# A two-layer hybrid trunk on one core: buffers on multiples of 128 bytes, head norms by Ln and Exp, a scan in another order

## The chip, the cores and the metric

The kernel runs on 1 of the 8 cores of a Trainium2 chip. The metric is the device time of one execution in microseconds, the median of several runs. Its engines: TensorE (PE; PEld are its weight loads), VectorE (DVE), ScalarE (ACT), GpSimd (POOL), SyncE (SP), which issues nearly all DMAs.

## What is computed

The reference has 256 latent and 256 context tokens of width 1,024 (here T = 512 columns, feature-major), and two layers. Each layer is `h += g1 * mixer(modulate(rms_norm(h)))`, then `h += g2 * relu(u @ w1)^2 @ w2`, with shift, scale and gate from `silu(c) @ w_mod`. Cut to what matters here:

```python
# layer 0 mixer: Fourier groups beside a bidirectional Mamba-2 scan, 4 groups g of 6 heads r, chunks of 128 tokens
cb     = einsum("bclgn,bcsgn->bclsg", cc, bc)                 # C.B of a chunk, shared by a group's heads
y_diag = einsum("bclsgr,bcsgrp->bclgrp", cb[..., None] * decay, xdt)
states = einsum("bcsgn,bcsgrp->bcgrpn", bc, xdt * decay_to_end[..., None])
h      = h * chunk_decay + state                              # carried over the chunks, both directions
y_off  = einsum("bclgn,bcgrpn->bclgrp", cc, h_enter) * exp(a_cum)
y      = rms_norm_per_group((y_diag + y_off + d_skip * xs) * silu(z)) * norm_g
out    = concatenate([fourier, y]) @ w_out                    # 2,048 -> 1,024
# layer 1 mixer: windowed attention and neighbourhood attention on projections, after
q, k   = rms_norm(q, per head of 64), rms_norm(k, per head of 64)
```

## The kernel before, in words

A script (`script()`) writes down a list of steps; every engine walks the same list and emits its own part of each step, so that the list is the order of every engine's queue. Between the engines stand counted semaphores. Every engine works strictly in this order, and a step whose wait isn't met holds up all that stands behind it on its engine.

*Products.* A float32 product is done as three passes of rounded halves: `w_hi*x_hi + w_hi*x_lo + w_lo*x_hi`. A weight tile is 1,024 x 128 (8 k tiles), so a product is 24 matmuls of 128x128 on 512 or 256 columns (`product`, L1506; the first two of a stage run interleaved by k in `pair_product`, L1513). SP loads tile u into `raw`, ScalarE copies it to `w_hi` (L839), VectorE subtracts for `w_lo` (L1094), both two products ahead, as the first thing of a product's step. The layer's input stands in `a_hi`/`a_lo`, the second operand (hidden values, second half of the mixer) in `b_hi`/`b_lo`. Results go to two PSUM banks in turn.

*Layer 0.* Projections of group 0 and the Fourier tiles, then the scan, group by group (163 to 525 us in the trace). In a group, eight slots (`slot(n)`) hold one product each, five of the next group's convolution inputs and three of z; in group 3, which has no successor, z in slots 0 to 2, nothing in slot 3, and then the output products outA 0 to 3. Around the slots stand the steps of the scan. `toks` turns tokens to rows (L1679, L1680). `cb` makes C.B of one chunk (L1694) and VectorE multiplies it with both masks into `cbm` (L1306). `seg` is the decay of one direction: six transposes (L1703), six Relu and one Exp into `ey` on ScalarE (L983, L986), times `cbm` on VectorE (L1312). `state`: GpSimd scales `xw` (two buffers, L827), TensorE multiplies (L1688), VectorE carries it on in `hent` (L1296, or L1298 and L1301). `yoff` takes the entering state (L1715; L1323, L1328), `y` the diagonal part (L1728, L1732), `yt` takes y down into `mixF` (L1338). `ysum`, `yrec`, `yrow`, `ynorm` normalise the group before (L1741, L995, L1352, L1749, L1360). Work of a convolution (taps L1242, L1245; L965; L1258) is placed by `gemm()` ahead of the next slot. States, cb, ysum, yoff and the head statistics take the PSUM banks 3 and 7 in turn (`B_AUX`), each only after its last user has been read.

*Mixer splits.* `mixF` has 16 tiles: 4 Fourier tiles and 3 of each group. `("mixsplit", 0)`, in the first turn of group 3, makes `a_hi`/`a_lo` of tiles 0 to 7 in one go (L1018, L1370), `("mixsplit", 1)`, after outA 6, `b_hi`/`b_lo` of tiles 8 to 15.

*Layer 1.* 18 projection products, q on 256 columns (8), k and v on 512 (5 each) (991 to 1089 us). Behind each, one slot later, `hstat`: a matmul sums the squares of a head (L1806), ScalarE takes `Sqrt` (L1002), VectorE the reciprocal (L1349); two slots later `hnorm` multiplies (L1425), and three later `rot` and, once, `dup` (L1827, L1440), the doubling of the window keys. Then attention, output product, MLP.

*MLPs.* Four passes of 8 ff1 products on `a` and 8 ff2 products on `b`: 512 columns in layer 0, 256 in layer 1.

*Buffers.* `place()` puts one buffer after another, each rounded up to 32 bytes, from byte 16512. `c0` is 8,224 bytes long, so that what follows it begins at 32 over a multiple of 128.

## Time and profile before

| | |
|---|---|
| median of 3 runs | 1374.86 us (1373.34 to 1379.74) |
| the profiled execution, its time | 1377.91 us |
| its span | 1376.1 us |
| granted TensorE clock, mean over the span | 0.961 |
| busy: PE, PEld | 1268.3 us, 1009.4 us |
| busy: DVE, ACT, POOL | 772.6 us, 506.3 us, 79.2 us |

The median says what the kernel takes; the profile is of one execution and says where. Its span runs from the first to the last instruction, and its own time is 1.8 us longer. TensorE's granted clock has two levels, 1 (2.4 GHz) and one half; a stretch's figure is the mean. A busy engine's time is counted as pieces, and matmuls overlap, so that busy time doesn't say how much could be saved; the waits do.

### The profile page before, as it was taken

The page shows a single profiled execution, that of the slowest core. Times are in us where ns is not written, and L with a number is a line of the kernel's source. Part 1 is how long each engine was busy: PE and PEld are TensorE (multiplying, and loading weights), DVE is VectorE, ACT ScalarE, POOL GpSimd, SP SyncE. Part 2 cuts the span into 40 slices and gives each one's busy share as a digit, 9 for nine tenths or more (in the row PEclk, how much of TensorE's full clock was granted, in tenths as well). Part 3 has the DMA queues.
Part 4 walks back from the last instruction along what each step waited for, and adds up shares of the span by engine and source line. Part 5 has one row for each costly group of instructions (what it writes and reads, how often), then busy time and mean ns, then how long its engine had stood idle before and what let it go on. Part 6 is the DMA issues. An engine that isn't in the chain of part 4 may idle for free.

```text
span 1376.1 us, 18731 instructions
## 1 busy us (share of the span) xinstructions
PE 1268.3 (92%) x7212; PEld 1009.4 (73%) x7212; DVE 772.6 (56%) x1203; ACT 506.3 (37%) x879; POOL 79.2 (6%) x70
## 2 busy tenths in 40 slices
PE   5799889899899899899999999999799799899998
PEld 1566667677677787677777777777587558899998
DVE  2644368586685555364353353343465796757664
ACT  2431144363444532341122122221543485534442
POOL 0000000101001002300000000004100002100000
PEclk9899999899899999899999999999899899999999
DMA  9456011111011112343444353443133202355553
GB/s 385 167 210 256 19 47 61 46 47 61 32 61 47 42 66 83 135 145 124 160 160 160 122 182 140 146 157 136 59 105 130 75 2 80 140 180 184 181 181 125
DMA packets 41531, 166.56 MB, mean 121 GB/s; under 512 B 4480, under 2 KB 6656, under 8 KB 38400
## 3 DMA queue, kind: packets, MB, share of 16 engines
q1 hardware_dynamic: 41040, 164.45, 33.5%
q10 hardware_dynamic: 432, 1.32, 0.2%
q8 instruction: 38, 0.62, 0.2%
q14 instruction: 21, 0.17, 0.0%
...
## 4 chain that ended last, share of the span: by engine, by line
PE 75%; DVE 12%; ACT 6%; issue 3%; DMA 3%; SPq 0%; DVEq 0%; ACTq 0%
PE ps L1506 53%; PE ps L1513 8%; PE ps L1529 3%; ACT ey L983 1%; DVE cacc L1245 1%; PE ps L1703 1%; DVE sm L1458 1%; DMA raw<-in_w_ff 1%; PE ps L1669 1%; DMA mring<-in_w_mod 1%; PE ps L1728 1%; PE ps L1715 1%; ACT u L889 1%; DMA xload<-in_ctx 1%; PE ps L1732 1%
## 5 line engine op out<-in xcount | busy, mean ns | idle before, releaser
L1506 PE MATMUL ps<-a_hi,w_hi 128*128 128x512 f32 (+1 forms) x880 | 330.2, 375 | 0.0
L839 ACT ACTIVATE w_hi<-raw 128x1024 fp32r<-128x1024 f32 x206 | 217.2, 1056 | 281.6 <-DMA raw<-in_w_ff 217.7
L1506 PE MATMUL ps<-a_hi,w_lo 128*128 128x512 f32 (+1 forms) x880 | 314.6, 357 | 0.0
L1506 PE MATMUL ps<-a_lo,w_hi 128*128 128x512 f32 (+1 forms) x880 | 314.5, 357 | 0.0
L1094 DVE TENSOR_TENSOR w_lo<-raw,w_hi 128x1024 fp32r<-128x1024 f32 x206 | 253.1, 1229 | 87.7 <-ACT w_hi L839 86.8
L1506 PEld LDWEIGHTS ps<-a_hi,w_hi 128*128 128x128 f32 x880 | 168.9, 192 | 38.3 <-ACT hr L1038 7.5
L1506 PE MATMUL ps<-b_hi,w_hi 128*128 128x512 f32 (+1 forms) x560 | 193.9, 346 | 0.0
L1506 PE MATMUL ps<-b_hi,w_lo 128*128 128x512 f32 (+1 forms) x560 | 192.0, 343 | 0.0
L1506 PE MATMUL ps<-b_lo,w_hi 128*128 128x512 f32 (+1 forms) x560 | 191.3, 342 | 0.0
L1506 PEld LDWEIGHTS ps<-a_lo,w_hi 128*128 128x128 f32 x880 | 168.7, 192 | 26.2 <-issue 2.6
L1506 PEld LDWEIGHTS ps<-a_hi,w_lo 128*128 128x128 f32 x880 | 168.0, 191 | 24.6
L1506 PEld LDWEIGHTS ps<-b_hi,w_hi 128*128 128x128 f32 x560 | 105.2, 188 | 23.0 <-issue 10.0
L1506 PEld LDWEIGHTS ps<-b_hi,w_lo 128*128 128x128 f32 x560 | 105.1, 188 | 13.9
L1506 PEld LDWEIGHTS ps<-b_lo,w_hi 128*128 128x128 f32 x560 | 105.2, 188 | 12.9
L1408 DVE SCALAR_TENSOR_TENSOR hT<-ps,mod,hT 128x256 f32<-128x256 f32 x96 | 43.3, 479 | 105.0 <-PE ps L1506 104.8
L1397 DVE TENSOR_TENSOR hq<-hr 128x512 f32<-128x512 f32 (+1 forms) x64 | 35.5, 555 | 103.3 <-ACT hr L1038 103.2
L1038 ACT ACTIVATE hr<-ps 128x512 f32<-128x512 f32 (+1 forms) x64 | 31.3, 488 | 161.8 <-PE ps L1506 115.6
L1513 PE MATMUL ps<-a_hi,w_hi 128*128 128x512 f32 (+1 forms) x192 | 70.1, 365 | 14.6 <-DVE a_lo L1184 12.5
L983 ACT ACTIVATE ey<-ps,acum 128x128 f32<-128x128 f32 x192 | 52.9, 374 | 53.9 <-PE ps L1703 53.3
L1529 PE MATMUL ps<-mring,sil 128*32 128x384 f32 (+1 forms) x448 | 57.3, 594 | 16.3 <-DMA mring<-in_w_mod 8.5
L1513 PE MATMUL ps<-a_lo,w_hi 128*128 128x512 f32 (+1 forms) x192 | 67.4, 351 | 0.0
L1513 PE MATMUL ps<-a_hi,w_lo 128*128 128x512 f32 (+1 forms) x192 | 67.1, 350 | 0.0
...
## 6 DMA issues: line engine op xcount, KB each, us to landing
raw<-in_w_ff SPq DMA_DIRECT2D x128, 512.0 KB, 3.4
...
```

The source lines that it names most:

```text
L839: nc.scalar.activation(w_hi[:, u % RING, :, :], raw[:, u % RING, :, :], ACT.Copy).then_inc(hi_done, 1)
L889: nc.scalar.activation(u32[:, f % 2, SEQ * i:SEQ * i + SEQ], nt[:, f % 2, SEQ * i:SEQ * i + SEQ], ACT.Identity, bias=mod[:, st[1], sh, i:i ...
L983: nc.scalar.activation(ey[:, di, r, :], ps[:, b + r // 3, P * (r % 3):P * (r % 3) + P], ACT.Relu, scale=-1.0, bias=acum[:, st[3], head_col ...
L1038: nc.scalar.activation(hr[:, m % 2, 0:ntok], ps[:, b, 0:ntok], ACT.Relu)\
L1094: v.tensor_tensor(w_lo[:, u % RING, :, :], raw[:, u % RING, :, :], w_hi[:, u % RING, :, :].bitcast(F32), ALU.subtract).then_inc(lo_done, 1)
L1245: v.scalar_tensor_tensor(out=acc, in0=cpad[:, n % 2, :, w:w + SEQ], scalar=convwT[:, w, t:t + 1], in1=acc, op0=ALU.mult, op1=ALU.add).then ...
L1397: v.tensor_tensor(hq[:, m % 2, 0:ntok], hr[:, m % 2, 0:ntok], hr[:, m % 2, 0:ntok], ALU.mult).then_inc(hq_done, 1)
L1408: ins = v.scalar_tensor_tensor(out=hs, in0=ps[:, b, SEQ * i:SEQ * i + SEQ], scalar=mod[:, L, 5 * KT + m, i:i + 1], in1=hs, op0=ALU.mult, o ...
L1458: v.tensor_reduce(sm[:, 3, i % 3, :], ps[:, b:b + 2, :], AX, ALU.max).then_inc(signal(dve_seq), 1)
L1506: ins = mm(out_ap, w_[:, n % RING, k, :], x_[:, k, 0:ntok], start=(k == 0 and j == 0), stop=(k == KT - 1 and j == 2))
L1513: ins = mm(outs[i], w_[:, tiles_[i] % RING, k, :], x_[:, k, 0:ntok], start=(k == 0 and j == 0), stop=(k == KT - 1 and j == 2))
L1529: ins = mm(ps[32 * q:32 * q + 32, b, 0:width], sil32[:, kk, :], mring[:, slot, width * q:width * q + width], start=(kk == 0), stop=(kk == ...
```

## The change

- `place()` rounds to 128 bytes, and `pick` in `c0` is 32 wide, so that every buffer begins at a multiple of 128. `zt` shares the place of `mrow`.
- Head norm factors are `exp(-0.5 * ln(mean + eps))`, both on ScalarE, and not `Sqrt` and a reciprocal on VectorE.
- `cb` is one step a group: four matmuls into one bank, one pass on VectorE, at the end of the group before. `cbm` holds all four chunks.
- The six states stand in a row around `seg b`, all ahead of slot 1, on three banks (3, 7 and 6) and four `xw` buffers (two of them lie in `ycomb`). `ysum` takes bank 2. The last `yt` of a group stands ahead of slot 6.
- The mixer splits are a step for each tile. Tiles 0 and 1 of the first half go to a new buffer `mixE` on the place of `cpad` and `cacc`, and the products take a list of operands (`operands`, not shown).

```diff
-    pick = np.zeros((P, 2 * QUADS))
+    pick = np.zeros((P, PICK_W))
...
+PICK_W = 32
+C0_A = 4 * P + PICK_W
...
-        def states(n):
-            for d, ch in STATES[n:n + 2]:
+        def states(i, n):
+            for d, ch in STATES[i:i + n]:
                 s.append(("state", g, d, ch))
+
+        def mixsplits(half, *tiles):
+            if g == G - 1:
+                s.extend(("mixsplit", half, f) for f in tiles)
         ch = SCAN_F
         if g == 0:
             s += [("toks", g, c_) for c_ in ch]
-        s += [("cb", g, ch[0]), ("seg", g, "f", ch[0])]
+            s.append(("cb", g))
+        s.append(("seg", g, "f", ch[0]))
         slot(0)
         if g:
             s.append(("ysum", g - 1))
-        states(0)
+        states(0, 3)
         s.append(("seg", g, "b", ch[0]))
-        states(2)
+        states(3, 3)
         if g:
             s.append(("yrec", g - 1))
+        mixsplits(0, 0)
         slot(1)
         if g:
-            s.append(("yrow", g - 1))
-        states(4)
-        if g:
-            s.append(("ynorm", g - 1))
+            s += [("yrow", g - 1), ("ynorm", g - 1)]
+        mixsplits(0, 1)
         for n in range(NCH):
             if n < NCH - 1:
-                s += [("cb", g, ch[n + 1]), ("seg", g, "f", ch[n + 1])]
+                s.append(("seg", g, "f", ch[n + 1]))
+            mixsplits(0, *((), (4,), (6, 7), ())[n])
             if n:
                 s.append(("yt", g, ch[n - 1]))
             s.append(("yoff", g, ch[n]))
             slot(2 + n)
             if n < NCH - 1:
                 s.append(("seg", g, "b", ch[n + 1]))
+            mixsplits(0, *((), (5,), (), ())[n])
             s.append(("y", g, ch[n]))
-            if g == G - 1 and n == 0:
-                s.append(("mixsplit", 0))
+            mixsplits(0, *((2, 3), (), (), ())[n])
+        s.append(("yt", g, ch[-1]))
         slot(6)
-        s.append(("yt", g, ch[-1]))
         if g < G - 1:
             s += [("toks", g + 1, c_) for c_ in ch[:2]]
+            s.append(("cb", g + 1))
             slot(7)
             s += [("toks", g + 1, c_) for c_ in ch[2:]]
         s.append(("ygate", g))
...
     s.append(("ysum", G - 1))
     gemm("outA", 4)
     s.append(("yrec", G - 1))
+    mixsplits(1, 0, 1)
     gemm("outA", 5)
     s += [("yrow", G - 1), ("ynorm", G - 1)]
+    mixsplits(1, 2, 3)
     gemm("outA", 6)
-    s.append(("mixsplit", 1))
+    mixsplits(1, 4, 5)
     gemm("outA", 7)
+    mixsplits(1, 6, 7)
...
-        elif k in ("state", "cb", "ysum", "hstat"):
-            n_var += k in ("ysum", "hstat")
-            job(st, B_AUX[n_aux % 2], freed={"state": ("ent_done", nk), "ysum": ("var_done", n_var),
-                                             "hstat": ("var_done", n_var)}.get(k))
+        elif k == "ysum":
+            n_var += 1
+            job(st, B_TR, freed=("var_done", n_var))
+        elif k == "state":
+            job(st, (B_AUX + (B_Y,))[(nk - 1) % 3], freed=("ent_done", nk))
+        elif k == "cb":
+            job(st, B_AUX[0])
+        elif k == "hstat":
+            n_var += 1
+            job(st, B_AUX[n_aux % 2], freed=("var_done", n_var))
...
-                at[0] += (size + 31) // 32 * 32
+                at[0] += (size + 127) // 128 * 128
...
+        mrow_at = at[0]
         mrow = place("mrow", [P, MI0 * P])
+        zt = place("zt", [P, T], offset=mrow_at)
...
-        cbm = place("cbm", [P, 2, P])
+        cbm = place("cbm", [P, NCH, 2, P])
         ycomb = place("ycomb", [P, 2, GX])
+        mixE = place("mixE", [P, 2, 2, T], F32R, offset=at[0])
...
+        xws = [xw[:, 0, :], xw[:, 1, :], ycomb[:, 0, :], ycomb[:, 1, :]]
+        mix_hi = [mixE[:, 0, k, :] if k < 2 else a_hi[:, k, :] for k in range(KT)], [b_hi[:, k, :] for k in range(KT)]
+        mix_lo = [mixE[:, 1, k, :] if k < 2 else a_lo[:, k, :] for k in range(KT)], [b_lo[:, k, :] for k in range(KT)]
...
-                    if n >= 2:
-                        pool.wait_ge(*filled(st_l[n - 2]))
-                    pool.tensor_tensor(heads(xw[:, n % 2, :]), heads(xdt[:, di, ch, :]),
+                    if n >= 4:
+                        pool.wait_ge(*filled(st_l[n - 4]))
+                    if n % 4 >= 2 and g:
+                        pool.wait_ge(*filled(("y", g - 1, SCAN_F[-1])))
+                    pool.tensor_tensor(heads(xws[n % 4]), heads(xdt[:, di, ch, :]),
...
-                    nc.scalar.activation(rms_of(st), ps[:, b, 0:odd_tokens[st[1:]]], ACT.Sqrt, scale=1.0 / HD,
+                    nc.scalar.activation(rms_of(st), ps[:, b, 0:odd_tokens[st[1:]]], ACT.Ln, scale=1.0 / HD,
                                          bias=eps[:, 0:1]).then_inc(signal(var_done), 1)
+                    act.wait_ge(*latest())
+                    nc.scalar.activation(rms_of(st), rms_of(st), ACT.Exp, scale=-0.5).then_inc(signal(hs_done), 1)
                 elif k == "mixsplit":
-                    hi = (a_hi, b_hi)[st[1]]
-                    if st[1]:
-                        high(unit[early] + AHEAD)
-                    for last_read in readers(st):
-                        act.wait_ge(*last_read)
-                    for f in range(KT):
-                        t = KT * st[1] + f
-                        act.wait_ge(mix_done, t + 1)
-                        if st[1] == 1 and f == 0:
-
-                            act.wait_ge(mix_done, 2 * KT)
-                            for q in y_jobs(G - 1, SCAN_F[-1]):
-                                act.wait_ge(*filled(q))
-                        nc.scalar.activation(hi[:, f, :], mixF[:, t, :], ACT.Copy).then_inc(signal(mixhi_done), 1)
+                    _, half, f = st
+                    if st == ("mixsplit", 0, 0):
+                        act.wait_ge(xbc_done, 5 * G)
+                    elif st == ("mixsplit", 0, 2):
+                        act.wait_ge(*filled(("gemm", "z", G * XT - 1)))
+                    elif st == ("mixsplit", 1, 0):
+                        for q in y_jobs(G - 1, SCAN_F[-1]):
+                            act.wait_ge(*filled(q))
+                    act.wait_ge(mix_done, KT * half + f + 1)
+                    nc.scalar.activation(mix_hi[half][f], mixF[:, KT * half + f, :], ACT.Copy).then_inc(signal(mixhi_done), 1)
...
-                    v.tensor_tensor(cbm[:, :, :], ps[:, b, None, 0:P].broadcast_to([P, 2, P]), masks, ALU.mult).then_inc(freeing(st), 1)
+                    v.tensor_tensor(cbm[:, :, :, :], ps[:, b, :].rearrange("p (c l) -> p c l", c=NCH).unsqueeze(2).broadcast_to([P, NCH, 2, P]),
+                                    masks.unsqueeze(1).broadcast_to([P, NCH, 2, P]), ALU.mult).then_inc(freeing(st), 1)
...
-                elif k == "hstat":
-                    dve.wait_ge(var_done, rms_n[st])
-                    v.reciprocal(rms_of(st), rms_of(st)).then_inc(signal(rstd_done), 1)
...
-                    hi, lo = ((a_hi, a_lo), (b_hi, b_lo))[st[1]]
-                    if st[1]:
-                        low(unit[early] + AHEAD)
-                    for f in range(KT):
-                        t = KT * st[1] + f
-                        dve.wait_ge(mixhi_done, t + 1)
-                        dve.wait_ge(*latest())
-                        v.tensor_tensor(lo[:, f, :], mixF[:, t, :], hi[:, f, :].bitcast(F32), ALU.subtract).then_inc(signal(split_done), 1)
+                    _, half, f = st
+                    dve.wait_ge(mixhi_done, KT * half + f + 1)
+                    dve.wait_ge(*latest())
+                    v.tensor_tensor(mix_lo[half][f], mixF[:, KT * half + f, :], mix_hi[half][f].bitcast(F32), ALU.subtract).then_inc(signal(split_done), 1)
...
-                    dve.wait_ge(rstd_done, rms_n[("hstat",) + st[1:]])
+                    dve.wait_ge(hs_done, qk_n[st[1:]] + 1)
...
-                    _, g, ch = st
+                    g = st[1]
+                    pe.wait_ge(xbc_done, 5 * g + 2)
                     b = jobs[st][0]
                     if free_before[st]:
                         pe.wait_ge(*emptied(st))
-                    mm(ps[:, b, 0:P], xbc[:, g % 2, 0, P * ch:P * ch + P], xbc[:, g % 2, 1, P * ch:P * ch + P], start=True, stop=True).then_inc(filling(st), 1)
+                    for ch in range(NCH):
+                        ins = mm(ps[:, b, P * ch:P * ch + P], xbc[:, g % 2, 0, P * ch:P * ch + P], xbc[:, g % 2, 1, P * ch:P * ch + P], start=True, stop=True)
+                    ins.then_inc(filling(st), 1)
```

VectorE's instructions in the first turn of group 1, from state 4 on (`hent` the states, `ey` the decay, `rcol` yrec, `cacc` the taps of a convolution, `mixF` with `vec` ynorm), before:

```order
L1298 TENSOR_TENSOR hent<-hent,dt_tot 128x384
L1301 TENSOR_TENSOR hent<-hent,ps 128x384
L1352 RECIPROCAL rcol<-rcol 128x4
L1242 TENSOR_SCALAR cacc<-cpad,vec 128x512
L1245 SCALAR_TENSOR_TENSOR cacc<-cpad,vec,cacc 128x512 x4
L1094 TENSOR_TENSOR w_lo<-raw,w_hi 128x1024
L1298 TENSOR_TENSOR hent<-hent,dt_tot 128x384
L1301 TENSOR_TENSOR hent<-hent,ps 128x384
L1298 TENSOR_TENSOR hent<-hent,dt_tot 128x384
L1301 TENSOR_TENSOR hent<-hent,ps 128x384
L1360 SCALAR_TENSOR_TENSOR mixF<-mixF,vec,ps 128x512 x3
L1306 TENSOR_TENSOR cbm<-ps,c_55 128x256
```

and with the change, from the second decay on (states 1 to 3 stand ahead of it):

```order
L1342 TENSOR_TENSOR ey_87<-ey_87,cbm 128x768
L1327 TENSOR_TENSOR hent<-hent,dt_tot 128x384
L1330 TENSOR_TENSOR hent<-hent,ps 128x384
L1327 TENSOR_TENSOR hent<-hent,dt_tot 128x384
L1330 TENSOR_TENSOR hent<-hent,ps 128x384
L1327 TENSOR_TENSOR hent<-hent,dt_tot 128x384
L1330 TENSOR_TENSOR hent<-hent,ps 128x384
L1379 RECIPROCAL rcol<-rcol 128x4
L1271 TENSOR_SCALAR cacc<-cpad,vec 128x512
L1274 SCALAR_TENSOR_TENSOR cacc<-cpad,vec,cacc 128x512 x4
L1124 TENSOR_TENSOR w_lo<-raw,w_hi 128x1024
L1387 SCALAR_TENSOR_TENSOR mixF<-mixF,vec,ps 128x512 x3
```

Two of the six states stood behind the reciprocal, the taps and the w_lo of slot 1, and cbm of the next chunk behind them; now all six stand ahead of the reciprocal, and there is no cbm.

ScalarE in group 3, behind the zt of the second z product (`ey` the decays, `a_hi<-mixF` the splits), before:

```order
L941 ACTIVATE zt<-ps 128x512
L983 ACTIVATE ey_87<-ps,acum 128x128 x6
L986 ACTIVATE ey_87<-ey_87 128x768
L1018 ACTIVATE a_hi<-mixF 128x512 x8
L983 ACTIVATE ey_86<-ps,acum 128x128 x6
L986 ACTIVATE ey_86<-ey_86 128x768
L983 ACTIVATE ey_86<-ps,acum 128x128 x6
L986 ACTIVATE ey_86<-ey_86 128x768
L983 ACTIVATE ey_87<-ps,acum 128x128 x6
```

and with the change:

```order
L973 ACTIVATE zt<-ps 128x512
L1015 ACTIVATE ey_88<-ps,acum 128x128 x6
L1018 ACTIVATE ey_88<-ey_88 128x768
L1048 ACTIVATE a_hi<-mixF 128x512 x2
L1015 ACTIVATE ey_87<-ps,acum 128x128 x6
L1018 ACTIVATE ey_87<-ey_87 128x768
L1048 ACTIVATE a_hi<-mixF 128x512
L1015 ACTIVATE ey_87<-ps,acum 128x128 x6
L1018 ACTIVATE ey_87<-ey_87 128x768
L1048 ACTIVATE a_hi<-mixF 128x512
L1015 ACTIVATE ey_88<-ps,acum 128x128 x6
L1018 ACTIVATE ey_88<-ey_88 128x768
```

The eight splits stood in one block between two decays; now two stand there, and the others one or two behind each decay (two have gone ahead, to `mixE`).

ScalarE in the odd projections, a v product and the statistics of the q product before it, before:

```order
L839 ACTIVATE w_hi<-raw 128x1024
L954 ACTIVATE vT<-ps 128x512
L1002 ACTIVATE nt<-ps,eps 128x256
L839 ACTIVATE w_hi<-raw 128x1024
L945 ACTIVATE kT<-ps 128x512
L949 ACTIVATE sq<-ps 128x512
```

and with the change:

```order
L870 ACTIVATE w_hi<-raw 128x1024
L986 ACTIVATE vT<-ps 128x512
L1034 ACT_TABLE_LOAD
L1034 ACTIVATE nt<-ps,eps 128x256
L1037 ACT_TABLE_LOAD
L1037 ACTIVATE nt<-nt 128x256
L870 ACTIVATE w_hi<-raw 128x1024
L977 ACTIVATE kT<-ps 128x512
L981 ACTIVATE sq<-ps 128x512
```

One `Sqrt` has become a table load, an Ln, a table load and an Exp; so it is for all 13.

## Rows read from the trace of the kernel before

**Rows 1.** The page, engines: busy us, share of the span, instructions.
```profile
PE 1268.3 (92%) x7212; PEld 1009.4 (73%) x7212; DVE 772.6 (56%) x1203; ACT 506.3 (37%) x879; POOL 79.2 (6%) x70
```

**Rows 2.** Table by stretch: length, busy us of each engine (x instructions), granted clock, DMA share, GB/s.
```profile
163.00:247.00 84.00, 75.06 (x437) 60.16 (x438) 60.62 (x97) 37.31 (x85) 7.49 (x8) 0.98 0.14 47
247.00:333.00 86.00, 77.44 (x440) 62.03 (x439) 62.09 (x98) 40.08 (x85) 6.17 (x6) 0.94 0.15 52
333.00:420.00 87.00, 78.29 (x437) 62.55 (x436) 61.65 (x97) 40.06 (x85) 6.18 (x6) 0.92 0.14 48
420.00:525.00 105.00, 94.88 (x517) 76.05 (x516) 62.66 (x100) 48.84 (x94) 3.54 (x4) 0.95 0.17 58
...
991.00:1089.00 98.00, 90.62 (x459) 74.68 (x459) 63.90 (x61) 42.13 (x72) 0.00 (x0) 0.98 0.35 118
```

**Rows 3.** TensorE's waits, whole run: what waited <- releaser: us, times, longest.
```profile
PE ps L1694 <- DVE hent L1301: 11.7, 4, 3.7
...
PE ps L1679 <- DVE mixF L1338: 5.5, 3, 1.8
...
PE ps L1715 <- DVE cbm L1306: 4.7, 3, 1.6
PE ps L1688 <- ACT rcol L995: 4.6, 3, 1.5
PE ps L1703 <- ACT ey L983: 4.5, 1, 4.5
...
PE ps L1513 <- DVE hT L1104: 2.5, 1, 2.5
PE ps L1827 <- DVE kdup L1440: 2.5, 1, 2.5
```

**Rows 4.** Timeline of TensorE, group 1: start, us, engine, line, operation [idle before <-releaser].
```profile
268.79 1.46 PE L1688 MATMUL ps<-xw,btok 128*128 128x384 f32 x4
273.87 0.80 PE L1694 MATMUL ps<-xbc 128*128 128x128 f32 x2 [3.63 <-DVE hent L1301]
...
275.74 1.32 PE L1715 MATMUL ps<-hent,xbc 128*128 128x384 f32 x2
```

**Rows 5.** Table by stretch, three short pieces; the granted clock stands ahead of the DMA share.
```profile
273.30:276.70 3.40, 2.83 (x11) 2.53 (x11) 3.16 (x6) 0.66 (x3) 0.00 (x0) 0.51 0.03 5
358.60:365.50 6.90, 6.05 (x17) 4.86 (x18) 5.68 (x10) 3.85 (x9) 0.00 (x0) 0.51 0.00 0
...
1044.70:1048.10 3.40, 3.40 (x11) 2.36 (x12) 1.56 (x2) 0.00 (x0) 0.00 (x0) 0.51 0.00 1
```

**Rows 6.** Timeline of TensorE, first MLP: 1st and 24th matmul of an a and a b product.
```profile
608.01 0.39 PE L1506 MATMUL ps<-a_hi,w_hi 128*128 128x512 f32 x1
...
613.22 0.39 PE L1506 MATMUL ps<-a_hi,w_lo 128*128 128x512 f32 x1
...
631.79 0.40 PE L1506 MATMUL ps<-b_hi,w_hi 128*128 128x512 f32 x1
...
637.16 0.40 PE L1506 MATMUL ps<-b_hi,w_lo 128*128 128x512 f32 x1
```

**Rows 7.** Table by stretch, one turn of group 1.
```profile
292.33:304.81 12.48, 10.90 (x73) 8.65 (x72) 11.39 (x19) 7.07 (x17) 0.00 (x0) 1.00 0.14 43
```

**Rows 8.** Groups by shape, VectorE: busy us, mean ns | idle before; one pass of a state.
```profile
L1301 DVE TENSOR_TENSOR hent<-hent,ps 128x384 f32<-128x384 f32 x16 | 8.9, 554 | 0.6
```

**Rows 9.** Timeline of ScalarE, group 3: the splits of the first half.
```profile
454.16 4.25 ACT L1018 ACTIVATE a_hi<-mixF 128x512 fp32r<-128x512 f32 x8
```

**Rows 10.** One line's instructions, the head reciprocals: shortest/median/longest ns.
```profile
L1349 DVE RECIPROCAL nt<-nt x13: 1743/1753/3353, 996.6 to 1085.9; 128x256 f32<-128x256 f32 x8, 128x512 f32<-128x512 f32 x5
```

**Rows 11.** Groups by shape, ScalarE: the table load of dt's Ln.
```profile
L903 ACT ACT_TABLE_LOAD x1 | 1.3, 1283 | 0.0
```

**Rows 12.** Timeline of ScalarE, odd projections: two k slots, each at its first copy.
```profile
1065.32 0.60 ACT L945 ACTIVATE kT<-ps 128x512 f32<-128x512 f32 x1 [3.50 <-PE ps L1506]
...
1071.64 0.60 ACT L945 ACTIVATE kT<-ps 128x512 f32<-128x512 f32 x1 [3.72 <-PE ps L1506]
```

44 lines of the change are left out of this document (24 added, 20 removed).

## The prediction

> **What bounds the kernel now.** I read the page first: TensorE is busy for 92% of the span [rows 1], so only what shortens its own work, or the time in which it waits, can pay. The table by stretch shows where it waits: in the scan (163 to 525 us, the four head groups) busy time falls short by some 36 us, in the odd projections (991 to 1089) by 7 [rows 2]. The list of TensorE's waits names the causes [rows 3]: in the scan the cb product waits 11.7 us in four waits for a state's copy on VectorE, the next group's transposes 5.5 us for the y tile, yoff 4.7 us for the cb bank, the states 4.6 us for ScalarE's ysum; later once 4.5 us behind the mixer splits, once 2.5 us at the start of outB, once 2.5 us at the doubling of the keys. The timeline shows the largest in its place in group 1 [rows 4], and pieces of time around such waits have a granted clock of 0.51 [rows 5]: the lower level, 1.2 instead of 2.4 GHz.
>
> **(a) Aligned buffers.** `a_hi`, `a_lo`, the weights and `hT` already began at multiples of 128 bytes; from `vec` on, nearly everything began 32, 64 or 96 bytes behind one, `b_hi` and `b_lo` by 32. In one pass of the first MLP an `a` product has 23 steps from 608.01 to 613.22, 226.5 ns each; a `b` product 23 steps from 631.79 to 637.16, 233.5 ns each [rows 6]. Shape, weights, clock and what the other engines do are alike, so I put the 7 ns on the buffer. It holds for 4 x 8 ff2 and 8 outB products of 24: 960 matmuls, 6.7 us, all on the path. The second MLP's 256-column products are paced by weight loads, whose buffers were aligned: nothing. For the other misplaced operands (mring, ey, hent, prob) no aligned twin stands in the trace; the bounds are nothing and, at 7 ns for some 400 wide ones, 3 us; I take nothing, as most are short. VectorE's and ScalarE's own times I leave as they are: they are off the path mostly, and between nothing and a gain there.
>
> The Trainium skill (SBUF — State Buffer, section Door 1, on the DMA port swizzle) gives SBUF lines of 16 bytes; 32 is a multiple of that, so by this rule the move changes nothing and the sum is 6.7 us smaller. Here [rows 6] speak against it.
>
> **(b) The scan.** Removed: the ysum bank ahead of the states (ysum now takes B_TR), the three cb products behind the states (cb is made once a group, ahead of slot 7 of the group before), yoff's wait for a cb bank, and the transposes' wait, as the last y tile is now taken down ahead of slot 6. These are the first four of [rows 3]: 11.7 + 5.5 + 4.7 + 4.6 = 26.5 us.
>
> What is late next? In group 1 yoff, with slot 2 behind it, began at 275.7, behind states 5 and 6 (268.8) and the 3.6 us wait [rows 4]. Now all six states stand ahead of slot 1. VectorE carries a state on with two passes of 0.55 us [rows 8], 3.3 us for the last three, which queue behind the second ey product. That product moves up by the 1.5 us that ysum cost, less the 0.7 of a third state; so VectorE is through at about 267, and with it the reciprocal that yrow needs. Slot 1 ends at about 266, so yrow may wait 1 us, and yoff starts at about 268: 7 to 8 us sooner. In the turns after that, TensorE was busy 10.9 us in the turn at 292 and waited the rest of 12.5 [rows 7]; VectorE's own turn by its widths (two ey 1.9, y 0.9, yoff 1.6, xbc 0.7, taps 3.7, w_lo 1.2) is 10.0, so the cover is thin. For yrow and such edges I put back 1.2 us a group, 4.8 us. The wide cbm is one pass of 1,024 columns for four of 256, no more than before and off the path; GpSimd's work is the same, only earlier, in four buffers.
>
> The clock: the pieces at 273.3 and 358.6 held 2.83 and 6.05 us of TensorE's work at 0.51 [rows 5]. They lie at the cb wait of group 1 and of group 2; without the wait I expect the full clock there, which gives half of that back, 4.4 us. Pieces at the states, where work is light with or without waits, I leave. Sum of (b): 26.5 - 4.8 + 4.4 = 26.1 us.
>
> **(c) Splits in pieces.** In group 3 eight a_hi copies, 4.25 us, stood between two ey steps on ScalarE [rows 9], and TensorE waited 4.5 us for the second. Now two stand there and one behind each ey. That turn has no product as cover: ey (some 2.5 us) and a split still come between two seg, so part stays; of 4.5 I take 2 us. At outB the last residual no longer queues behind eight b_lo passes: the wait of 2.5 us goes. The waits per tile inside the first pair are covered, as each k takes 6 matmuls, 1.4 us, and a split 0.5 us on ScalarE and 0.7 on VectorE.
>
> **(d) Head norm factors.** Removed: 13 reciprocals on VectorE of 1.75 to 3.35 us [rows 10]. Added on ScalarE: 13 exponentials of about 0.55 us and, by the order, a table load ahead of each Ln and each Exp, 26 of 1.283 us [rows 11] (one at the head of attention goes): 40 us on an engine busy 42 of 98 [rows 2]. It must be checked by slot. A k slot lasts 6.3 us and ScalarE idles 3.7 of it [rows 12]; 1.28 + 1.28 + 0.6 + 0.1 = 3.3 are added: it fits, with 0.4 to spare. A q slot lasts 3.3 us and ScalarE needs 5.2: it falls back by 1.9, in at most two slots in a row, and the v slot behind them and weights made two products ahead take that up. So I cost the loads at nothing, hidden by products. Gained on the path: the doubling of the keys queued behind a reciprocal, 1.2 us of the 2.5 go, and of the half-clock piece there (3.4 us [rows 5]) 0.6; ahead of attention a reciprocal of 3.35 and two norms become load, Ln, load, Exp and one norm, 0.7. Sum 2.5 us.
>
> The Trainium skill (ScalarE: Activation LUTs, section Table sets) has Ln and Exp in one set, so that Ln then Exp is one load; in this program the Ln of dt, behind an Exp, has its own load [rows 11], and the order shows one for each. By the page's 2.7 us a load, ScalarE would need 8.8 us in a k slot and bind it; the trace has 1.283.
>
> **Sum.** 6.7 + 26.1 + 2 + 2.5 + 2.5 = 39.8 us. The profiled execution took 1377.9 us (its span is 1376.1), which makes 1338; it lies 3.0 us over the median of the runs, 1374.9, so **1335 us**.
>
> **Rivals.** *R1, the buffers do nothing*: what makes `b` products slower would be something else in their place. For it, that no other row tells aligned from misplaced; against it, [rows 6]. 1335 + 6.7 = 1342. The rule on 16-byte lines above gives the same time. *R2, the waits only move*: VectorE, in strict order, becomes the bound where a turn has a convolution (10.0 us against TensorE's 10.5), and yrow or yoff inherits the wait for the last state. For it, the thin margin; against it, the reciprocals, cb and ysum no longer chain the engines. Half of (b) lost is 1348, all of it 1361. *R3, slower: the loads bind ScalarE in the odd projections.* Each slot would then wait for two loads and an Exp: 26 x 1.283 + 13 x 0.55 = 40.5 us in front of TensorE, and as TensorE waits in each slot, the stage's products (8 x 2.9 + 10 x 5.5 = 78 us) would run in part at the lower clock as in [rows 5]; half of them adds 39. 1335 + 40.5 gives 1376, with 10 to 39 for the clock 1386 to 1415. It decides where ScalarE needs more than a k slot's 6.3 us; I have 5.9. *R4, no such change*: the order shows all pieces in place, so only the clock could hide them; within R2.
>
> **How the numbers follow.** A measurement of this kernel can tell about 0.5% from no change: under 1368.0 is faster, over 1381.7 slower. Forecast 0.71, R1 0.10, R2 0.13, R3 0.04, other 0.02. All but R3 and the unnamed are faster, save a rest of R2 joined by a part of R3's waits: faster 0.91, same 0.04, slower 0.05. Low end: none of the 4.8 put back, the 3 us of (a), and 7 us more of clock: 1320. High end: R2 whole, 1360.
>
> **What would show it.** `b` products step at 227 ns, or (a) is wrong. TensorE's list has no wait of cb for hent and none of the transposes for mixF, and a group takes 75 to 79 us. In the odd projections ScalarE is busy over 75 us, yet no wait of TensorE ends in it. The forecast is wrong if a group still takes over 82 us, or if ScalarE ends TensorE's waits there.

## The result and the profile after

The changed kernel takes **1321.76 us**, median of 4 runs (1320.65 to 1324.72), the kernel before 1374.95 us. The ratio is 0.9607 with a 95% interval of 0.9589 to 0.9626: faster by 53 us, where the prediction had 40. The profiled execution took 1322.42 us, its span is 1320.6 us, and the granted clock is 0.974 on the mean.

The page of the changed kernel, engines, as [rows 1]:

```profile
PE 1245.9 (94%) x7212; PEld 1000.6 (76%) x7212; DVE 744.2 (56%) x1178; ACT 546.0 (41%) x917; POOL 79.3 (6%) x70
```

The number of matmuls is the same, and still TensorE is busy for 22 us less. That is the first sign of where the time came from: not from the waits alone.

The table by stretch of the changed kernel, with the columns of [rows 2]. The stretches are shifted so that each holds the same products as there: four groups of the scan, then the odd projections.

```profile
163.60:238.30 74.70, 73.13 (x443) 59.70 (x444) 61.34 (x95) 37.48 (x85) 9.11 (x10) 1.00 0.16 52
238.30:312.20 73.90, 72.74 (x440) 59.31 (x439) 61.91 (x95) 40.26 (x85) 6.29 (x6) 1.00 0.18 59
312.20:387.20 75.00, 73.60 (x437) 59.84 (x436) 61.23 (x94) 40.24 (x85) 6.33 (x6) 0.98 0.17 56
387.20:487.20 100.00, 94.50 (x519) 76.39 (x518) 62.34 (x99) 48.88 (x94) 2.03 (x2) 0.97 0.19 62
941.00:1035.80 94.80, 89.13 (x459) 73.49 (x459) 36.06 (x49) 80.58 (x108) 0.00 (x0) 1.00 0.37 122
```

Group 1 took 86.0 us and takes 73.9. Of these 12.1 us, waits are 7.4 (length less busy time: 8.56 before, 1.16 now), and 4.7 is busy time (77.44, now 72.74) for the same 440 matmuls, at a clock of 1.00 for 0.94. Group 2 shows the same: 12.0 us, 7.3 of them waits and 4.7 busy time. The prediction had a group at 75 to 79 us; these two take 73.9 and 75.0.

TensorE's waits in the changed kernel, whole run (what waited, the releaser, us, times, longest), as [rows 3]:

```profile
PE ps L1775 <- DVE rcol L1379: 3.7, 3, 1.4
...
PE ps L1729 <- ACT ey L1015: 1.6, 1, 1.6
PE ps L1758 <- DVEq L1360: 1.6, 1, 1.6
...
PE ps L1853 <- DVE kdup L1463: 0.8, 1, 0.8
```

The first four waits of [rows 3] are gone, 26.5 us. New are 3.7 us of yrow for the reciprocal, and in group 3, behind the first splits, 1.6 for the second ey (4.5 before) and 1.6 for VectorE's queue.

The pieces at half clock, between the scan's start and the end of outB. In the kernel before there were eight; the table of those pieces, without the two whose like stands in [rows 5] (273.4 to 276.8 and 358.7 to 365.5, busy 2.93 and 6.05 us):

```profile
188.00:191.40 3.40, 3.35 (x11) 2.75 (x12) 1.53 (x3) 1.18 (x5) 0.00 (x0) 0.50 0.00 0
256.30:263.10 6.80, 5.70 (x14) 3.71 (x15) 1.18 (x3) 3.63 (x9) 2.56 (x4) 0.50 0.00 0
...
341.60:348.40 6.80, 5.42 (x13) 3.52 (x14) 1.46 (x3) 3.63 (x9) 2.76 (x3) 0.50 0.02 4
...
430.40:433.80 3.40, 3.40 (x10) 2.18 (x9) 0.56 (x2) 0.94 (x4) 0.83 (x1) 0.50 0.00 0
457.70:464.50 6.80, 4.30 (x30) 3.57 (x30) 6.08 (x11) 5.59 (x16) 0.00 (x0) 0.50 0.00 0
525.90:529.40 3.50, 3.46 (x8) 2.81 (x9) 1.02 (x1) 0.53 (x1) 0.00 (x0) 0.51 0.00 0
```

and all that the changed kernel has there:

```profile
320.40:323.80 3.40, 3.40 (x9) 2.00 (x8) 2.60 (x4) 1.81 (x3) 2.11 (x2) 0.50 0.00 0
395.50:398.90 3.40, 3.40 (x9) 1.96 (x8) 3.10 (x5) 1.82 (x3) 2.03 (x2) 0.50 0.01 2
460.40:463.80 3.40, 3.40 (x9) 2.63 (x9) 1.22 (x1) 3.40 (x6) 0.00 (x0) 0.50 0.02 6
```

Eight pieces became three. TensorE's work in them was 34.6 us and is 10.2. At half clock work takes nearly twice its time (a step of 430 ns for 230 in gap_three, below), so that by estimate the pieces cost 17.3 us before and cost 5.1 now: 12.2 us won, where the prediction had 4.4. The three that are left have no wait ahead of them. Each begins 2.8 to 3.3 us after the start of a `ysum`, which is 24 matmuls of one column; the one ahead of 320.4 in the timeline:

```profile
317.12 2.73 PE L1767 MATMUL ps<-c,gate 128*128 128x1 f32 x24
```

Over the scan and outA as a whole (from product 9 to the middle of outB's first pair, with the wait in it) the two traces differ by 43.4 us, 27.5 of them waits and 15.9 busy time. Below, "scan and outA" is always this stretch.

A `b` product of the first MLP in the changed kernel, first and 24th matmul, as the lower half of [rows 6]:

```profile
587.22 0.39 PE L1529 MATMUL ps<-b_hi,w_hi 128*128 128x512 f32 x1
...
592.43 0.39 PE L1529 MATMUL ps<-b_hi,w_lo 128*128 128x512 f32 x1
```

23 steps in 5.21 us are 226.5 ns each, for 233.5 before.

ScalarE in a k slot of the odd projections, timeline of the changed kernel, as [rows 12]:

```profile
1018.41 0.60 ACT L977 ACTIVATE kT<-ps 128x512 f32<-128x512 f32 x1 [0.36 <-PE ps L1529]
1018.90 0.59 ACT L981 ACTIVATE sq<-ps 128x512 f32<-128x512 f32 x1
1019.51 1.28 ACT L1034 ACT_TABLE_LOAD   x1
1020.81 0.69 ACT L1034 ACTIVATE nt<-ps,eps 128x512 f32<-128x512 f32 x1
1021.52 1.28 ACT L1037 ACT_TABLE_LOAD   x1
1022.81 0.63 ACT L1037 ACTIVATE nt<-nt 128x512 f32<-128x512 f32 x1
1023.35 1.04 ACT L870 ACTIVATE w_hi<-raw 128x1024 fp32r<-128x1024 f32 x1
1024.76 0.60 ACT L977 ACTIVATE kT<-ps 128x512 f32<-128x512 f32 x1 [0.36 <-PE ps L1529]
```

The slot lasts 6.35 us and ScalarE idles 0.36 of it, where it idled 3.7: it fits, by a hair.

Following the products one by one through both traces, the changed kernel is ahead by 8.7 us behind group 0, 20.8 behind group 1, 32.8 behind group 2, 42.1 in the middle of outB's first pair, 44.1 at the first MLP, 50.0 at the odd projections, 55.1 at outO and 55.5 at the end of the span. At the start of the scan it is 1.3 us behind; half-clock pieces of the prologue lie otherwise there, as they do from kernel to kernel in all the runs below.

### The profile page after: what moved, and what is told of

The parts are those of the page before. It is cut to its first block, busy times and chain, and to the rows that moved or that the text cites. A ratio compares the mean times of both kernels' runs of the same rounds, so it can differ in the third digit from the quotient of the medians.

```text
span 1320.6 us, 18748 instructions
## 1 busy us (share of the span) xinstructions
PE 1245.9 (94%) x7212; PEld 1000.6 (76%) x7212; DVE 744.2 (56%) x1178; ACT 546.0 (41%) x917; POOL 79.3 (6%) x70
## 4 chain that ended last, share of the span: by engine, by line
PE 85%; DVE 7%; ACT 4%; DMA 3%; issue 2%; SPq 0%; DVEq 0%; ACTq 0%
PE ps L1529 59%; PE ps L1536 8%; PE ps L1552 3%; PE ps L1729 2%; PE ps L1754 1%; DVE sm L1481 1%; PE ps L1692 1%; DMA mring<-in_w_mod 1%; PE ps L1741 1%; PE ps L1711 1%; PE ps L1758 1%; ACT u L920 1%; PE ps L1767 1%; DMA xload<-in_ctx 1%; ACT ey L1015 1%
## 5 line engine op out<-in xcount | busy, mean ns | idle before, releaser
L1529 PE MATMUL ps<-a_hi,w_hi 128*128 128x512 f32 (+1 forms) x868 | 321.9, 371 | 0.0
L1529 PE MATMUL ps<-a_lo,w_hi 128*128 128x512 f32 (+1 forms) x868 | 308.9, 356 | 0.0
L1529 PE MATMUL ps<-a_hi,w_lo 128*128 128x512 f32 (+1 forms) x868 | 308.8, 356 | 0.0
L1529 PEld LDWEIGHTS ps<-a_hi,w_hi 128*128 128x128 f32 x868 | 165.2, 190 | 37.8 <-issue 8.5
L1529 PEld LDWEIGHTS ps<-a_lo,w_hi 128*128 128x128 f32 x868 | 165.2, 190 | 24.7 <-issue 1.0
L1529 PEld LDWEIGHTS ps<-a_hi,w_lo 128*128 128x128 f32 x868 | 164.9, 190 | 23.8
L1529 PEld LDWEIGHTS ps<-b_hi,w_lo 128*128 128x128 f32 x560 | 106.2, 190 | 12.2
L1536 PE MATMUL ps<-a_hi,w_hi 128*128 128x256 f32 (+1 forms) x188 | 68.6, 365 | 12.0 <-DVE a_lo L1214 11.9
L1552 PE MATMUL ps<-mring,sil 128*32 128x384 f32 (+1 forms) x448 | 57.9, 600 | 15.7 <-DMA mring<-in_w_mod 8.1
L1536 PE MATMUL ps<-a_lo,w_hi 128*128 128x256 f32 (+1 forms) x188 | 66.3, 352 | 0.0
L1536 PE MATMUL ps<-a_hi,w_lo 128*128 128x256 f32 (+1 forms) x188 | 66.0, 351 | 0.0
```

The source lines that it names most:

```text
L1529: ins = mm(out_ap, w_[:, n % RING, k, :], (x_[k][:, 0:ntok] if type(x_) is list else x_[:, k, 0:ntok]), start=(k == 0 and j == 0), stop=(k ...
L1536: ins = mm(outs[i], w_[:, tiles_[i] % RING, k, :], (x_[k][:, 0:ntok] if type(x_) is list else x_[:, k, 0:ntok]), start=(k == 0 and j == 0) ...
L1552: ins = mm(ps[32 * q:32 * q + 32, b, 0:width], sil32[:, kk, :], mring[:, slot, width * q:width * q + width], start=(kk == 0), stop=(kk == ...
```

## Experiments

All kernels below were timed against the kernel before, on one chip for each set. Where two of them are compared, it is by their ratios, 0.001 of which is 1.4 us; the changed kernel's ratio is 0.9607.

### a_alone: the buffers alone, on the kernel before

```diff
-                at[0] += (size + 31) // 32 * 32
+                at[0] += (size + 127) // 128 * 128
```

> The kernel before with every buffer rounded up to 128 bytes and nothing else changed. Theory (the buffers are worth the b products alone): b products step at 227 ns for 233.5, 960 x 7 ns = 6.7 us, so 1374.9 - 6.7 = 1368. Rival 1 (the scan's and the norms' operands also gained by their place, which would explain part of the 13 us that the change brought beyond my sum): 1355 to 1362. Rival 2 (the place of a buffer does nothing, the b products sped up for another reason): 1375, steps still 233.5.

Measured: 1371.16 us, ratio 0.9953 (0.9938 to 0.9968), so 6.5 us (4.4 to 8.5). A `b` product of the first MLP starts its first matmul at 629.87 and its 24th at 635.09, 227 ns a step. Both rivals fall: the buffers do something, and no more than that.

### a_offsets: three operands off the multiple, on the changed kernel

```diff
+        a_lo = place("a_lo", [P, KT, T], F32R, shift=96)
+        b_hi = place("b_hi", [P, KT, T], F32R, shift=64)
+        b_lo = place("b_lo", [P, KT, T], F32R, shift=32)
```

(`shift` adds to the buffer's place, the next one is rounded up to 128 again.)

> The changed kernel with three operands moved off a multiple of 128 bytes: a_lo by 96, b_hi by 64, b_lo by 32; a_hi stays. The trace shows each operand's own step. Theory 1 (anything off a multiple of 128 costs): matmuls on a_lo, b_hi and b_lo at 512 columns step at 233 to 234 ns, those on a_hi at 227; some 670 + 320 + 320 of them x 7 ns = 9.2 us, 1331. Theory 2 (a multiple of 64 is enough): b_hi stays at 227, a_lo and b_lo rise, 6.9 us, 1328.7. Theory 3 (these places do nothing): 1321.8.

Measured: 1327.47 us, ratio 0.9656 (0.9630 to 0.9681), 6.7 us more than the changed kernel. The same `b` product in its timeline:

```profile
589.49 0.40 PE L1529 MATMUL ps<-b_hi,w_hi 128*128 128x512 f32 x1
...
594.79 0.40 PE L1529 MATMUL ps<-b_hi,w_lo 128*128 128x512 f32 x1
```

230.4 ns a step; an `a` product has 231.3. So the third theory falls, and the first holds in its sign but not in its picture: the step isn't set by each operand's own place, since those on `a_hi`, which stayed at 0, slowed down with the others, and neither product reached 233.5. The second theory is not settled, because `b_hi` (64) and `b_lo` (32) slowed together.

What nobody had asked stands in the second MLP. With 256 columns, the `b` product numbered 200 takes 2.71 us for its 23 steps here, 117.8 ns each, as in the kernel before (117.7); in the changed kernel it has 120.0, and so it has in a_alone, where nothing but the places differs from the kernel before. **Off the multiple, the narrow products are faster.** From outO to the end a_offsets wins back 3.7 of the 7.8 us that it had lost.

### d_undone and d_double: the head norm factors

```diff
-  nc.scalar.activation(rms_of(st), ps[...], ACT.Ln, scale=1.0 / HD, ...)
-  nc.scalar.activation(rms_of(st), rms_of(st), ACT.Exp, scale=-0.5)
+  nc.scalar.activation(rms_of(st), ps[...], ACT.Sqrt, scale=1.0 / HD, ...)
+  v.reciprocal(rms_of(st), rms_of(st))
```

> The changed kernel with the head norm factors by Sqrt on ScalarE and a reciprocal on VectorE, as before. My sum had the change at 2.5 us, the two traces differ by 5.1 us over the odd projections and the head of attention (a wait of the doubling 1.7 shorter, one ahead of attention 0.6 shorter, the rest clock). Theory (all of that is the change of the factors): 1321.8 + 5.1 = 1327. Rival (my 2.5 us, the rest was the clock's luck): 1324. Rival (nothing, the loads cost what the reciprocals did): 1322.

Measured: 1330.3 us, ratio 0.9659 (0.9646 to 0.9672), 7.2 us more than the changed kernel. Its waits in the odd projections and ahead of attention:

```profile
PE ps L1868 <- DVE kT L1449: 5.0, 1, 5.0
PE ps L1854 <- DVE kdup L1464: 2.5, 1, 2.5
```

The doubling's wait is 2.5 us again, and a piece at half clock follows it (997.1 to 1000.5) that the changed kernel doesn't have. Followed by products, it falls behind by 3.2 us at this place and by 0.7 more up to outO. It is behind by 1.1 us already at the first MLP, with the same program up to there, because its trace has a piece at half clock behind the ysum in group 1, where the changed kernel's trace has none:

```profile
243.12 2.73 PE L1768 MATMUL ps<-c,gate 128*128 128x1 f32 x24
```

```profile
246.20:249.60 3.40, 3.40 (x8) 1.78 (x7) 2.33 (x5) 2.00 (x3) 1.78 (x2) 0.51 0.00 0
```

Some 3.9 us are the factors' own in the traces; 7.2 with an interval of some 3 us on either side is the runs' figure. The theory's 5 us lies within that, and both rivals lie below it.

```diff
   nc.scalar.activation(rms_of(st), rms_of(st), ACT.Exp, scale=-0.5)
+  nc.scalar.activation(rms_of(st), rms_of(st), ACT.Ln)
+  nc.scalar.activation(rms_of(st), rms_of(st), ACT.Exp)
```

> The changed kernel with a second Ln and a second Exp behind the first pair of each head statistic, same values: two more table loads and two more passes, 2 x 1.28 + 1.2 = 3.8 us more of ScalarE for each of the 13. Theory (the loads are hidden only as long as a slot has room: a k slot of 6.3 us had 5.9 in it, a q slot of 3.3 had 5.2): now k slots need 9.7, q slots 8.4 to 9.0, v slots 2.3, together some 127 us against a stage of 92, so 35 us slower and up to 20 more by the clock: 1357 to 1377, with the weights' w_hi ending TensorE's waits. Rival (ScalarE has plenty of room, its loads overlap with its other work): 1322 to 1326.

Measured: 1361.07 us, ratio 0.9884 (0.9867 to 0.9901), 38 us more. TensorE's waits in this stage:

```profile
PE ps L1836 <- ACT sq L981: 10.4, 5, 3.3
PE ps L1843 <- ACT vT L986: 8.1, 1, 8.1
PE ps L1871 <- DVE kT L1452: 7.5, 1, 7.5
```

The slots' arithmetic holds on both sides of its limit: at 5.9 us in a 6.3 us slot no wait of TensorE in the odd projections ends in ScalarE, and at 9.7 the stage grows by 36 us, where 35 and some clock had been worked out. A load is 1.283 us in every record of both kernels. The Trainium skill (ScalarE: Activation LUTs, section What ACT_TABLE_LOAD costs) makes its 2.7 us of a load of about 1.283 us and of a drain of about 1.38. The first figure agrees with the trace. The drain doesn't show: in the k slot above the load follows the Activate before it by 0.02 us, and the Ln follows the load as closely. The same page (section Table sets) has Ln and Exp in one set; here each Ln and each Exp has its own load.

### states_split: the states in their old places

```diff
-        states(0, 3)
+        states(0, 2)
         s.append(("seg", g, "b", ch[0]))
-        states(3, 3)
+        states(2, 2)
...
-            s += [("yrow", g - 1), ("ynorm", g - 1)]
+            s.append(("yrow", g - 1))
+        states(4, 2)
+        if g:
+            s.append(("ynorm", g - 1))
```

> The changed kernel with the states in their old places: two, two, and the last two behind yrow; cb once a group, the banks and all else stay. Theory 1 (the order of the states was what made the large wait, and waits draw half-clock pieces after them): the 11.7 us that cb waited for the last state come back at yoff, with 0.6 us of clock for each us waited (before against changed, TensorE's busy time over the scan fell by 13.5 us and its waits by 25.6), so +12 to +19: 1334 to 1341 on a chip where the changed kernel takes 1322. Theory 2 (the wait comes back without any clock): +12, 1334. Rival (the chain over cb's bank was the cause, the order does nothing): 1322 to 1325.

Measured: 1347.52 us, ratio 0.9797 (0.9775 to 0.9819), 26 us more. Its waits, and its group 1 in the table by stretch:

```profile
PE ps L1744 <- DVE hent L1333: 15.8, 4, 4.7
...
PE ps L1778 <- DVE rcol L1382: 2.3, 3, 0.8
```

```profile
243.70:325.60 81.90, 76.46 (x439) 61.55 (x437) 61.43 (x95) 40.18 (x85) 5.88 (x6) 0.94 0.16 52
```

With cb made once a group the wait for the last state simply passes to yoff, and is longer than it was (15.8 for 11.7). TensorE is busy for 76.46 us with the work that takes 72.7 in the changed kernel: the clock has gone with it. At each of the four waits for the last state a piece at half clock begins, within the wait or just behind it (190.4, 268.9, 350.8, 432.7). Over the scan and outA this kernel takes 23.4 us more, 14.1 waits and 9.3 busy time. The first theory holds, 0.66 us beside each us waited for its 0.6; its total was too low because the wait came back longer. So **this one move, two states from behind yrow to ahead of slot 1, carries more than half of what the scan gained**, and two fifths of it is busy time, nearly all of that clock.

### yt_late: the last y tile behind slot 6

```diff
-        s.append(("yt", g, ch[-1]))
         slot(6)
+        s.append(("yt", g, ch[-1]))
```

> The changed kernel with the last yt of a group behind slot 6 again. Theory (the transposes wait for the y tile again, and the clock follows): 5.5 us of waits in three groups and 3 us of clock, +8.5, 1330. Rival 1 (waits alone): +5.5, 1327. Rival 2 (other waits at the group's end were what held it; VectorE is freer there now): 1322 to 1324.

Measured: 1327.04 us, ratio 0.9652 (0.9633 to 0.9671), some 6 us more. The wait is back to the tenth, and yet no piece at half clock has come behind it:

```profile
PE ps L1702 <- DVE mixF L1368: 5.5, 3, 1.8
```

Over the scan and outA it takes 4.2 us more and has two pieces at half clock, both behind a ysum, to the changed kernel's three. Rival 1: these waits cost themselves alone. Three waits of 1.8 us each, a full product on either side, drew no piece.

### gap_one and gap_three: waits put in by hand

```diff
+            if GAPS[n]:
+                s.append(("gap", g, n))
             s.append(("yoff", g, ch[n]))
...
+                    pool.wait_ge(*filled(gap_after[st]))
+                    for i in range(GAPS[st[2]]):
+                        pool.tensor_tensor(gapb[:, :], xdt[:, 0, 0, 0:256], xdt[:, 0, 1, 0:256], ALU.mult).then_inc(gap_seq, 1)
...
+                    pe.wait_ge(gap_seq, n_gap)
```

`GAPS` is (6, 0, 0, 0) in gap_one and (2, 2, 2, 0) in gap_three.

> The changed kernel with one added wait in each of the four groups: GpSimd runs six passes of 128x256 once the transposes ahead of the first yoff are done, and TensorE waits for them ahead of that yoff; no other engine waits. Each wait some 4 us, 16 us in all. Theory (idle time of TensorE costs it half-clock pieces besides, about 0.5 us for each us waited): +22 to +26, 1344 to 1348, with two or more pieces at 0.5 more in the scan, at the groups' heads. Rival (the clock pieces are independent of such waits): +16 or less, 1338.

> The same number of passes as in gap_one, but two ahead of each of the first three yoff of a group: twelve waits of some 1.3 us, 16 us in all, beside products on either side. Theory A (the sum of the waits draws the pieces): +22 to +26 again. Theory B (only a wait that stands where the work is light already does): +14 to +18, 1336 to 1340, and no more half-clock pieces than without. Part of the waits may be absorbed by what TensorE would otherwise have waited for.

Measured: gap_one 1354.41 us, ratio 0.9858 (0.9827 to 0.9890), 35 us more; gap_three 1362.59 us, ratio 0.9902 (0.9876 to 0.9928), 41 us more. GpSimd's passes are slower than I had taken them for, so that the waits are larger than planned, but they are alike in sum. Waits of gap_one:

```profile
PE ps L1761 <- POOL gapb L863: 27.1, 4, 7.4
```

and of gap_three:

```profile
PE ps L1761 <- POOL gapb L863: 26.0, 12, 2.4
```

Over the scan and outA, gap_one takes 32.1 us more than the changed kernel, of which 5.7 is TensorE's busy time; gap_three takes 38.5, of which 16.6 is. VectorE is busy 5 to 6 us longer than in the changed kernel in both, which doesn't tell the two apart. Two of the pieces at half clock of gap_one:

```profile
274.50:281.40 6.90, 2.90 (x6) 2.01 (x7) 6.27 (x8) 1.58 (x2) 3.71 (x4) 0.51 0.01 2
356.50:363.30 6.80, 2.99 (x6) 2.09 (x7) 6.17 (x8) 1.58 (x2) 3.52 (x4) 0.50 0.00 0
```

and two of the eleven of gap_three:

```profile
275.40:278.80 3.40, 3.40 (x9) 2.61 (x9) 3.40 (x5) 1.58 (x2) 0.00 (x0) 0.50 0.02 5
289.00:292.40 3.40, 3.40 (x10) 2.42 (x9) 3.03 (x7) 1.20 (x2) 0.00 (x0) 0.50 0.01 2
```

The timeline of gap_three behind its gap in group 1 shows what such a piece is:

```profile
274.49 0.91 PE L1761 MATMUL ps<-hent,xbc 128*128 128x384 f32 x2 [1.99 <-POOL gapb L863]
...
275.96 0.63 PE L1546 MATMUL ps<-a_hi,w_lo 128*128 128x512 f32 x1
276.39 0.63 PE L1546 MATMUL ps<-a_hi,w_hi 128*128 128x512 f32 x1
...
279.10 0.39 PE L1546 MATMUL ps<-a_lo,w_hi 128*128 128x512 f32 x1
279.33 0.40 PE L1546 MATMUL ps<-a_hi,w_lo 128*128 128x512 f32 x1
```

TensorE waits 2 us behind six short transposes, starts the product, and its matmuls step at 430 ns from 275.4 to 278.8 and at 230 behind that. In gap_one the theory had the sign and too high a price, 0.5 us for each us waited where 5.7 beside 27.1 is 0.2. Both theories of gap_three's expectation were too narrow: twelve short waits drew eleven pieces, in which TensorE worked all of their 37.7 us, and the kernel with four long ones has five pieces, in which it worked for 18.7 of 34.2 us; the rest was the wait itself, and half a clock costs nothing in a wait. Half of 37.7 and of 18.7, less the 5.1 us of the changed kernel, makes 13.8 and 4.3, near the 16.6 and 5.7 measured. Eleven of gap_three's twelve added waits have a piece right behind them, and at all four of gap_one's a piece begins within the wait. The same sum of waits cost 11 us more of busy time in small coins. So it is not the sum of the waits that sets this price here, but how many of them draw a piece and how much work lies in it.

### scan_only: what is left without buffers and factors

```diff
-                at[0] += (size + 127) // 128 * 128
+                at[0] += (size + 31) // 32 * 32
...
-PICK_W = 32
+PICK_W = 8
```

and the edit of d_undone.

> The changed kernel with its buffers back on multiples of 32 bytes, at the places that they had before, and the head norm factors back to Sqrt and reciprocal: of the change, the scan's order and the mixer splits in pieces are left. a_alone measured 6.5 us for the buffers, d_undone about 7 for the factors. Theory (the parts add): 0.9607 + 0.0047 + 0.0052 = 0.9706 of the kernel before, 1334.5 on a chip where that takes 1375, so that scan and splits are worth 40 us where my sum had 30.6. Rival (the parts need each other, the scan's gain rests in part on the places of its operands): over 1340.

Measured: 1333.07 us, ratio 0.9697 (0.9674 to 0.9720), 41.7 us less than the kernel before. Scan and outA take 322.4 us, against 322.0 in the changed kernel and 365.4 before, at the same waits and with the same three pieces. The parts add: 41.7 + 6.5 + 7.2 = 55.4, and 53 measured, within their intervals. My sum had 30.6 for what is left here. The scan's gain doesn't lean on its buffers' places.

### yrow_later, late_shift, shift_and_yrow: what is still to be had

yrow_later moves yrow and ynorm behind slot 2:

```diff
-            s += [("yrow", g - 1), ("ynorm", g - 1)]
...
             slot(2 + n)
+            if g and n == 0:
+                s += [("yrow", g - 1), ("ynorm", g - 1)]
```

> The changed kernel with yrow and ynorm of the group before behind slot 2 instead of slot 1. In the trace of the changed kernel TensorE waits 3.7 us in three waits for the reciprocal that yrow transposes. Theory (the wait is VectorE's queue, states ahead of the reciprocal, and a product more covers it): -3.7 us, 1318 on a chip where the changed kernel takes 1322, and fewer half-clock pieces if the waits drew them. Rival (ynorm's three passes then push VectorE's taps or w_lo, and the wait moves to them): 1321 to 1324.

Measured: 1324.02 us, ratio 0.9615 (0.9602 to 0.9628), no gain. The wait for rcol is gone and half of it stands elsewhere, at yoff. The other half is offset in the trace: all four ysums have a piece at half clock behind them, one more than in the changed kernel's, and that costs 1.7 us. One trace doesn't say whether that is chance:

```profile
PE ps L1741 <- DVE hent L1330: 1.9, 3, 0.6
```

late_shift lays the operands of outO and of the second MLP off the multiple, inside the same buffers:

```diff
+A_SH, B_SH = (0, 24), (8, 8)
+        a_late = [t[:, :, q:q + SEQ] for t, q in zip((a_hi, a_lo), A_SH)]
+        b_late = [t[:, :, q:q + SEQ] for t, q in zip((b_hi, b_lo), B_SH)]
```

> The changed kernel with the operands of the last output product and of the second MLP, all of 256 columns, placed off a multiple of 128 again, inside the same buffers: a_hi at 0, a_lo at 96, b_hi and b_lo at 32 bytes. Theory (a product of 256 columns is faster off the multiple: the a_offsets run has 116 to 118 ns for 120, the kernel before 116 to 119 on b): 960 matmuls on a x 2.6 ns + 768 on b x 2.3 ns = 4.3 us, 1317.7. Rival (it was something else in a_offsets): 1322, steps of 120.

Measured: 1322.71 us, ratio 0.9596 (0.9580 to 0.9612). The `b` product numbered 200, in late_shift:

```profile
1296.63 0.28 PE L1536 MATMUL ps<-b_hi,w_hi 128*128 128x256 f32 x1
...
1299.32 0.28 PE L1536 MATMUL ps<-b_hi,w_lo 128*128 128x256 f32 x1
```

and in the changed kernel:

```profile
1295.00 0.28 PE L1529 MATMUL ps<-b_hi,w_hi 128*128 128x256 f32 x1
...
1297.76 0.28 PE L1529 MATMUL ps<-b_hi,w_lo 128*128 128x256 f32 x1
```

117 ns a step for 120. From the first product of outO to the last of the MLP it gains 2.5 us of the 4.3 expected, which the intervals of the two ratios don't part from nothing; the steps do. Where the rest went stays open.

> Both edits at once. They touch different stages, so they should add: 1322 - 3.7 - 4.3 = 1314. If yrow_later gains nothing, 1318.

Measured: 1320.2 us in five runs (1319.62 to 1320.47), ratio 0.9586 (0.9573 to 0.9599). It has the lowest ratio of all, but its interval and that of the changed kernel overlap, so it isn't shown to be faster than that; in the trace its outO and second MLP are 3.6 us shorter, and the rest is not better.

## Why the prediction was right, and where it was off

The forecast was faster, 1335 us in a range of 1320 to 1360; the time is 1321.8, at the low edge. That it still lies inside is in part luck: the low end was made of 7 us more of clock (7.8 came), of the 4.8 us put back (3.7 were there) and of 3 us for other operands, of which a_alone shows nothing.

By its steps:

- **(a), 6.7 us.** Right: a_alone has 6.5, and the `b` products step at 227 ns. The rival R1 is out: an offset of 32 bytes cost 7 ns in 234. The Trainium skill (SBUF — State Buffer, section Door 1) has lines of 16 bytes, by which 32 would do no harm; a_alone and the steps speak against reading it so for TensorE's operands. What the sum missed is the other sign on narrow products, "nothing" in my text: 120 ns for the 117.7 of before in the `b` products of the second MLP, some 1.8 us lost by 768 matmuls, though the stage as a whole came out no longer. a_alone, late_shift and a_offsets show this sign too.
- **(b), waits.** Right in kind and size. The first four of [rows 3] went, 26.5 us, and I had 4.8 put back: yrow waits 3.7. The place was right too, yrow behind the reciprocal. states_split shows the order of the states to be the largest piece of it, and that the wait doesn't need cb's bank: it stands wherever the entering states are first asked for.
- **(b), the clock.** This is the step that was off, the one term that was much too small. I priced two pieces, those at the cb waits of groups 1 and 2, at 4.4 us; both went, 4.5. Three more stood behind waits that my own sum removes or shortens, and I gave them nothing: 188.0 behind group 0's cb wait, 457.7 behind the ey wait, 525.9 behind outB's. They went too, 5.6 us. The pieces at the states (256.3, 341.6, 430.4) I had left, "with or without waits", and that was half right: each stands behind a ysum. Group 1's is gone from this trace and group 2's is down to 3.4 us, 3.9 us in all; group 3's is where it was (395.5), and a new one stands behind the last ysum (460.4), 1.7 us lost. Together that is the 12.2 us. states_split, gap_one and gap_three show the link of waits and pieces: put waits back, and pieces come with them. They don't show it for the pieces behind a ysum, which have no wait ahead of them now. How many of those a trace has is in part chance: in the eight traces with the scan in the new order (yrow_later and shift_and_yrow differ in yrow alone) there are 2 (a_offsets), 3 (the changed kernel, scan_only) or 4 (d_undone, d_double, late_shift, yrow_later, shift_and_yrow), so that 1.7 us more or less of the 12.2 say nothing. Whether it is ysum's narrow matmuls that draw them wasn't tried.
- **(c), 4.5 us.** The ey wait fell from 4.5 to 1.6, 2.9 where I had 2, but 1.6 for VectorE's queue is new beside it; outB's wait for hT is gone as predicted, and with it the piece at 525.9, 1.7 us, counted above like that at 457.7. It wasn't tried alone.
- **(d), 2.5 us.** Hidden, as said: the slack of a k slot was to be 0.4 us and is 0.36, and d_double proves the limit. R3 is out. The gain was mis-sized, 5.1 us between the two traces, 3.9 by d_undone's trace and 7.2 by its runs: the doubling's wait fell by 1.7 for my 1.2, and its piece at half clock went whole, 1.7 for my 0.6.
- **R2** (the waits only move) came true for a seventh of the waits, the 3.7 us at yrow, and again in yrow_later, where moving that step too only handed the wait to the next: group 1 now has 1.2 us of waits in 73.9, group 2 has 1.4 in 75.0.

In sum, the two traces differ by 55.5 us, 15.7 beyond the sum of 39.8 (the medians by 53.2). Of these, 11.5 are busy time in scan and outA (15.9 for my 4.4; the pieces make 7.8 of the 11.5, the other 3.7 I can't name, and a_alone shows that they aren't the buffers), 1.3 waits there (27.5 for 21.7 + 2 + 2.5), 2.6 the odd projections with the head of attention, 1.6 small differences in the other stages, and 1.3 go off for the prologue. By the runs, the order of the states is worth 26 us and the place of the last yt 6 of the 41.7 that scan_only measures; cb in one step, the banks and the splits in pieces weren't tried one by one. Why the first half-clock pieces of the prologue lie now here, now there (its length differs by up to 2.9 us between kernels whose prologue is the same) stays open, and so does why 1.8 us of wait ahead of the transposes drew no piece where 2 us ahead of yoff did.
